# The second block's second mixer: a new order of its indexer, its latent attention and its output product

## The reference, cut to what matters

```python
def odd_mixer(x, w_in, q_norm_g, kv_norm_g, w_uq, w_ukv, w_o):
    qc, kc, vc, qi, ki, wi, cq, ckv, kr = split_cols(x @ w_in, ODD_SIZES)
    out_c = dsa_attention(qc(8 heads x 64), kc, vc, qi(4 x 64), ki, wi)
    q  = (rms_norm_2(cq, q_norm_g) @ w_uq)   # 8 heads x (64 + 32)
    kv = (rms_norm_2(ckv, kv_norm_g) @ w_ukv) # 8 heads x (64 + 64)
    q = concat([q[..., :64], rope(q[..., 64:], pos)])
    k = concat([kv[..., :64], rope(kr, pos) for every head])
    out_d = causal_block_attention(q, k, kv[..., 64:])
    return concat([out_c, out_d]) @ w_o
```

## Time and profile before

| | us |
|---|---|
| median of 3 runs | 2596.35 (2591.0 to 2599.19) |
| the profiled execution, its own time | 2602.1 |
| its span, first to last instruction | 2600.3 |
| PE busy in it | 2454.0 |
| DVE busy in it | 1727.7 |
| ACT busy in it | 1196.8 |
| mean granted clock of TensorE | 0.946 |

### The profile page before, as it was taken

One profiled execution on the slowest core, in us unless ns is written; L12 is line 12 of the kernel. 1 busy time (PEld: TensorE's weight loads), 2 busy tenths in 40 slices (PEclk: granted clock), 3 DMA queues, 4 the chain that ended last, 5 costly groups with the idle time before them and its releaser, 6 DMA issues.

```text
span 2600.3 us, 33971 instructions
## 1 busy us (share of the span) xinstructions
PE 2454.0 (94%) x14242; PEld 2109.2 (81%) x14242; DVE 1727.7 (66%) x2242; ACT 1196.8 (46%) x1493; POOL 98.7 (4%) x187
## 2 busy tenths in 40 slices
PE   6999999899999999999999999989999889899998
PEld 2778887767789999998899997867787767788776
DVE  4897776653656656655556655578787676588787
ACT  3212222343544444445444443466666544476565
POOL 0111111010000000000000000000000000000000
PEclk8999999999879999999899999999999886899999
DMA  6678787322114454456334543348887520298774
GB/s 270 220 236 265 263 267 249 123 87 77 65 65 163 172 194 168 167 194 224 109 144 177 191 162 113 102 161 301 315 315 300 208 97 23 103 350 323 274 301 187
DMA packets 80531, 502.23 MB, mean 193 GB/s; under 512 B 9621, under 2 KB 10725, under 8 KB 28513
## 3 DMA queue, kind: packets, MB, share of 16 engines
q1 hardware_dynamic: 59264, 424.71, 44.3%
q0 software_dynamic: 21088, 75.01, 9.1%
HBM read 498.63 MB, written 1.05 MB: 192 GB/s over the span
## 4 chain that ended last, share of the span: by engine, by line
PE 75%; DVE 14%; ACT 7%; issue 3%; DMA 1%; DVEq 0%; ACTq 0%; SPq 0%
PE bank L393 73%; DVE wl L1795 6%; ACT wh L1233 4%; DVE macc L1825 1%; PE bank L570 1%; ACT s L1318 1%; DVE f L1950 1%; DVE s L1941 1%; DMA raw<-in_wmod 1%; PE bank L1130 1%; DVE rs L1849 1%; DVE hl L1925 0%; DMA mring<-in_wmod 0%; ACT H L1327 0%; DVE tmpm L1918 0%
## 5 line engine op out<-in xcount | busy, mean ns | idle before, releaser
L1795 DVE TENSOR_TENSOR wl<-raw,wh 128x2048 fp32r<-128x2048 f32 x394 | 901.5, 2291 | 403.3 <-ACT wh L1233 400.8
L1233 ACT ACTIVATE wh<-raw 128x2048 fp32r<-128x2048 f32 x394 | 751.8, 1911 | 380.3 <-PE bank L393 379.0
L393 PE MATMUL bank<-hh,wh 128*128 128x258 f32 (+2 forms) x2200 | 694.5, 316 | 36.4 <-DVE wl L1795 18.4
L393 PE MATMUL bank<-hh,wl 128*128 128x258 f32 (+2 forms) x2200 | 678.8, 309 | 0.0
L393 PE MATMUL bank<-hl,wh 128*128 128x258 f32 (+2 forms) x2200 | 677.2, 308 | 0.0
L393 PEld LDWEIGHTS bank<-hh,wh 128*128 128x128 f32 x2200 | 424.9, 193 | 63.8 <-issue 18.0
L393 PEld LDWEIGHTS bank<-hl,wh 128*128 128x128 f32 x2200 | 425.8, 194 | 18.6
L393 PEld LDWEIGHTS bank<-hh,wl 128*128 128x128 f32 x2200 | 424.2, 193 | 19.2
L393 PE MATMUL bank<-wh,hh 128*128 128x512 f32 (+1 forms) x704 | 278.9, 396 | 5.2 <-DVE hl L2690 2.4
L393 PE MATMUL bank<-wh,hl 128*128 128x512 f32 (+1 forms) x704 | 274.3, 390 | 0.0
L393 PE MATMUL bank<-wl,hh 128*128 128x512 f32 (+1 forms) x704 | 274.3, 390 | 0.0
(11 more groups left out here) (421 smaller groups left out, 2760.1 us busy)
## 6 DMA issues: line engine op xcount, KB each, us to landing
raw<-in_wstream SPq DMA_DIRECT2D x394, 1024.0 KB, 4.9
mring<-in_wmod POOLq DMA_DIRECT2D x128, 512.0 KB, 4.6
raw<-in_wmod SPq DMA_DIRECT2D x8, 1024.0 KB, 9.3
X<-in_xT SPq DMA_DIRECT2D x1, 2048.0 KB, 12.5
bias<-in_nabias POOLq DMA_DIRECT2D x16, 128.0 KB, 2.5
c_sglg<-in_sglg POOLq DMA_DIRECT2D x1, 1024.0 KB, 5.2
c_sglb<-in_sglb POOLq DMA_DIRECT2D x1, 1024.0 KB, 7.4
out<-X SPq DMA_DIRECT2D x4, 256.0 KB, 2.2
```

The costliest lines, as they stand in the source:

```text
L393: return e.matmul(out, lhsT, rhs, start=start, stop=stop, skip_group_check=True)
L1233: e.activation(wh[i % NB][:], raw[i % NR][:], ACT.Copy).then_inc(*slab_high(i))
L1795: e.tensor_tensor(wl[i % NB][:], raw[i % NR][:], wh[i % NB][:].bitcast(F32), ALU.subtract).then_inc(*slab_low(i))
```

## The change

Packing. The columns of `w_uq` are reordered: four chunks of two heads' 64 unrotated parts (`od.qn`) and two chunks of four heads' rotated parts (`od.qr`), so `uq` takes 6 chunks instead of 8, and `ukvk` 4 instead of 8 (`od.kn`). The rotated key part is projected four times side by side, so that one rotation of 128 partitions serves it. The queries are rotated by one `rotate` over two chunks. The latent logits become two products into one bank, one of 64 rows (`qn`, `kn`) and one of 32 rows (`qr`, `kr`); `okf` goes. The mixer's tiles are now 80 + 12 + 4 + 4 + 24 (+ 4 empty) + 64, 12 slabs instead of 13.

Order. `ocq`, `ock`, `okr`, one `oqc` chunk and `okc` follow the indexer's columns, with selection steps between their tiles. The other three `oqc` chunks come after `ukvv`, with five attention steps in each (after tiles 1, 2, 4, 5, 7). All selection steps are run out before the first attention step (`pump(100)`). After the three chunks come 5 bare attention steps, then the transposes of the latent half of `Y` with a step after each, then 14 steps each behind two tiles of the half of w_o that needs only the latent half; the rest of w_o follows when the sparse half is done.

```diff
+OD_UNITS = (1, 2, 4, 5, 7)
@@ PE
+        def out_part(out, name, d, b, ks, first, last):
+            for k in ks:
+                w.wait_ge(dve_out, "turn l", name, k // 2)
+                wmm((out, d, k), b, hh[:, k, T:2 * T], hl[:, k, T:2 * T], k == first and (d > 5 or d % 2 == 0), k == last, out, d)
...
-            p(1, 11, "okr", 3)
-            p(2, 8, "ocq", 3)
-            p(1, 10, "ock", 3)
-            p(2, 0, "oqc", 1)
...
-            p(2, 2, "oqd", 1)
-            p(1, 4, "okc", 1)
+            p(2, 8, "ocq", pumps=True)
+            p(1, 10, "ock", pumps=True)
+            p(1, 11, "okr", pumps=True, middle=root_sum)
+            p(1, 0, "oqc", pumps=True)
             rotate(("rot", "kr"), od.kr[:].unsqueeze(1), act_out, "okr", 0)
+            p(1, 4, "okc", pumps=True)
...
+            q_part(4)
+            q_part(5)
+            for m in range(4):
+                q_part(m)
+                if m == 0:
+                    rotate(("rot", "qr"), od.qr, act_out, "uq", 5)
...
                 if kd == "la":
-                    w.wait_ge(dve_out, "okf")
-                    return mm(b[:, 0:n], od.qf[0:96, hd, P * qb:P * qb + P], od.kf[0:96, hd, 0:n], True, True)
+                    mm(b[:, 0:n], od.qn[r, hd // 2, q], od.kn[r, hd // 2, 0:n], True, False)
+                    r = slice(32 * (hd % 4), 32 * (hd % 4) + 32)
+                    return mm(b[:, 0:n], od.qr[r, hd // 4, q], od.kr[r, 0:n], False, True)
...
-            for _ in attention("od", OD, od.a, logits, values, (4, 5)):
-                pump(2)
-            for c in range(KC):
-                turn_out("od", od.Y, c)
-            out_proj("wo1", h_part, KC, ...)
+            pump(100)
+            st.units = attention("od", OD, od.a, logits, values, (4,))
+            p(3, 0, "oqc", m0=1, units=OD_UNITS)
+            pad()
+            attend(5)
+            for i in (2, 3):
+                turned(i, bank(("turn", "od", i), dve_out, "turn l", "od", i))
+                attend(1)
+            out_banks("wo1")
+            for d in range(6):
+                for k in (4, 6):
+                    part(d, where(d), k, k + 2)
+                    attend(1)
+            part(6, ends[0], 4, 6)
+            attend(1)
+            part(6, ends[0], 6, 8)
+            attend(1)
+            part(7, ends[1], 4, 6)
+            for i in (0, 1):
+                turned(i, bank(("turn", "od", i), dve_out, "turn l", "od", i))
+            part(7, ends[1], 6, 8)
+            sums_begin(2)
+            for d in range(KC):
+                part(d, where(d) if d < 6 else ends[d - 6], 0, 4)
+                if d > 1:
+                    sum_of(2, d - 2, "wo1", d - 2)
@@ ACT and DVE: the same order; DVE's loop over the 14 steps
+            for _ in range(14):
+                attend(1)
+                taken(2)
```

More of the change, by code:

```diff
@@ L429, in pad, with pad4 @@
                 st.tile += n
+        def pad4():
+            n = -st.tile % 4
+            order[-1].extend([None] * n)
+            st.tile += n
         def ended(ins, slab, last, key):
@@ L956, in h, with root_sum, p @@
                 return ("sp", 8, k)
-            def p(chunks, c0, key, steps=0):
-                for m in range(chunks):
+            def root_sum():
+                b = bank(("ossq",), dve_out, "omean")
+                for lo, n in ((0, 2), (2, 1)):
+                    for k in range(lo, lo + n):
+                        w.wait_ge(act_out, "osq", k)
+                        ins = mm(b[:, P * lo:P * lo + T], ones[:], od.lsq[:, k, :], k == lo, k == lo + n - 1)
+                ins.then_inc(*result("ossq"))
+            def p(chunks, c0, key, m0=0, pumps=False, units=(), middle=None):
+                for m in range(m0, m0 + chunks):
                     b = bank((key, m), act_out, key, m)
+                    st.kept.add(bank_of[key, m])
                     for k in range(KC):
@@ L963, in p @@
                         wmm(("oin", c0 + m, k), b[:, 0:T], hh[:, k, 0:T], hl[:, k, 0:T], k == 0, k == KC - 1, key, m)
-                    pump(steps)
-            st.selection = iter(())
+                        if pumps and k % 2:
+                            pump(1)
+                        if k in units:
+                            attend(1)
+                        if k == 3 and middle:
+                            middle()
+                    st.kept.remove(bank_of[key, m])
             p(1, 7, "oki")
@@ L1634, in odd_mixer, with root, high, p @@
             w.wait_ge(result, "moe 0")
-            def p(chunks, key, dst, scale=1.0, steps=0):
-                for m in range(chunks):
-                    taken(KC)
+            def root():
+                w.wait_ge(dve_out, "omean")
+                e.activation(rs[:], rs[:], ACT.Sqrt).then_inc(*act_out("oroot"))
+            def high():
+                for k in range(3):
+                    w.wait_ge(dve_out, "oc", k)
+                    e.activation(od.ch[:, k, :], od.cq[:, k, :], ACT.Copy).then_inc(*act_out("och", k))
+            def p(chunks, key, dst, scale=1.0, m0=0, pumps=False, units=0, middle=None):
+                for m in range(m0, m0 + chunks):
+                    taken(KC)
+                    if pumps:
+                        pump(4)
+                    attend(units)
+                    if middle:
+                        middle()
                     w.wait_ge(result, key, m)
                     e.activation(dst(m), banks[bank_of[key, m]][:, 0:T], ACT.Copy, scale=scale).then_inc(*act_out(key, m))
-                    pump(steps)
+            def query(m):
+                return od.qc[:, m, :]
             p(1, "oki", lambda m: od.ki[:])
@@ L2532, in odd_mixer @@
                                 ALU.add).then_inc(*dve_out("omean"))
-            for _ in range(2):
-                taken(KC)
-                pump(1)
+            pump(2)
             w.wait_ge(act_out, "oroot")
@@ L2566, in odd_mixer @@
+            pump(4)
+            for m in (4, 5, 0, 1, 2, 3):
                 taken(2)
+                if m == 0:
+                    behind()
+                    rotate(("rot", "qr"), od.qr)
                 pump(1)
-                if h % 2 and h > 1:
-                    rotate(("rot", h - 3), od.qf[:, h - 3:h - 1, :])
-            for h in range(8):
+            for m in range(4):
                 taken(1)
-                if h == 1:
-                    rotate(("rot", 6), od.qf[:, 6:8, :])
```

240 lines of the change are left out of this document (131 added, 109 removed).

## The result

The changed kernel takes 2615.83 us in the median (2598.06 to 2639.0, 10 runs), the kernel before 2595.39 beside it (2583.67 to 2609.94, 10 runs). The ratio is 1.0075, with a 95% interval of 1.0039 to 1.0112. The prediction was 2589.5, its range 2578 to 2604. A second measurement of the changed kernel gave 1.0113 [1.0038, 1.0188]. The profiled execution took 2608.53 us, its span is 2606.3.

A forecast was written before the change was run, and what follows sets the result against it. PE was taken as busy in 94% of the span, with DVE setting the pace before the attention. -20.4 us before the attention and +13.5 behind it take 6.9 off the median 2596.35: 2589.5 us, range 2578 to 2604.

The forecast's parts named there:

- Step 1, DVE's way: From DVE's copy of `ovw` to its first attention step: 43.8 us of work plus 4.4, reached 20.4 us earlier.
- The rival of a late start: Old DVE waits before the attention come back, up to 10 us, giving 2599.5; chance 0.14.
- My lower bound: DVE's earliest first attention step if there are no waits at all: 2124.5.
- Step 2, PE's work: PE's attention stage at the full clock: 61.7 us left from DVE's start; product pairs 0.42 on 128 keys, 0.63 on 256.
- Step 3(a) and (b), the waits: Attention stage waits: first exponentials 1.4 us; slab splits 5.3 in the second `oqc` chunk and 5.6 at tiles 128 and 144.
- The two of 2.8 at tiles 128 and 144: In the attention, slab splits between two loop steps leave PE waiting 2.8 us each time, 5.6 together.
- Step 3(d), the clock: In the attention, 10 to 15 us of PE's work runs at 1.2 GHz, costing 6 us more.
- The sum: -20.4 us before the attention, +13.5 behind it (97.4 to the last sum product, against 83.9): 6.9 off.
- The rival that came true: Attention stage stays at the half clock: +24 us over the whole stage, 2605 with two thirds slow; chance 0.16.
- the 8 us of standstills: In the half-clock rival's price, 8 of PE's 38 us of added work hide the split stalls.
- a cheap clock: Rival: clock and splits cost nothing in the attention, PE returns to 2.4 GHz at once; 6 us less, 2583.5; chance 0.20.
- Products side by side: Rival: the second latent product runs beside the first where row groups differ, 4.2 us less, 2585; chance 0.05.

The follow-up runs named there:

- `e_mask`: Changed kernel with every logit product on 128 rows, each head's key part in its own tile, zero elsewhere; 2589.98 us, 0.9964 of the kernel before.
- `e_rows`: Changed kernel with all logit products on 128 rows, two heads mixed in the logits (other values); 2585.44 us, 0.9953 of the kernel before.
- `e_96`: Changed kernel with all logit products on 96 rows from row 0, heads mixed; 2584.82 us, 0.9961 of the kernel before.
- `e_row0`: Changed kernel with logit products on as few rows as before but always from row 0, heads mixed; 2623.64 us, 1.0123 of the kernel before.
- `e_fill`: Changed kernel plus unused 128-row products, 40 in the first wait and four ahead of each unit's logits; 2613.61 us, 1.005 of the kernel before.

## Why the prediction was wrong, by its own steps

- **Step 1, DVE's way: right.** 48.2 us from the copy of `ovw` to the first attention instruction, forecast 48.1; five splits. The rival of a late start is out. (My lower bound is off by a little: 2078.6 + 43.8 + 2.4 of gaps is 2124.8, not 2124.5.)
- **Step 2, PE's work: the sizes were right at the full clock,** 0.42 and 0.63 per narrow product. What I didn't ask is why a second product should cost as much as the first. I took it for the price of a product; 0.2 of it is the change of rows, with a weight load that stands beside nothing. The way in and out, some 0.2 a step, I left out.
- **Step 3(a) and (b), the waits: half right.** PE's standstill in the second chunk was forecast at 5.3 and is 4.96, in its place and ended by an exponential. The first exponentials were forecast at 1.4 and are 1.35 (2108.97 to 2110.32). The two of 2.8 at tiles 128 and 144 don't show in the changed kernel, where PE at half the clock is always late; with the clock up `e_mask` has 2.29 and 3.00 there.
- **Step 3(d), the clock: this is the step that failed.** "With tiles between the steps I take 10 to 15 us of PE's work at 1.2 GHz." It was all of the stage, 108.6 us. I had read the earlier trace rows as a matter of how busy PE is and what stands around it: attention brought the clock back at 2163, so attention plus tiles would sooner. (The prediction calls it sparse attention; by the rows it was the latent one.) But the rows also say which products were which: those at 2152 to 2163 had 96 rows, those of 2178 to 2203, at 97% busy and 0.50, had 64. The change turned the first sort into the second sort and a third (32 rows). The clock fell at the end of the DVE-bound stage (0.98 in 2103 to 2109, 0.50 from 2109), and this mix of steps and tiles doesn't bring it back; with wide rows and the same steps and tiles it comes back (`e_rows`, `e_96`, `e_mask`).
- **The sum.** From the first attention step to the last sum product I forecast 97.4 us, bounds 92 to 103; measured 133.2. In `e_mask` it is 94.3 (2131.33 to 2225.6), so rows are 38.9 of it: 10 to 16 for the changes of rows, of which my sizes held 9.6 already, and 23 to 29 for the clock. That is the net of the standstills which slower work hides: PE is idle in the attention for 6.4 us here and 14.6 in `e_mask`, and its busy time is 102.2 against 54.05, 48.2 more, of which over 30 are the clock's. So one term decides: 3(d) was sized 6 where it is 23 at the least, and above 30 in PE's own work. Without the 9.6 my working would give 87.8 for `e_mask`; its 6.5 more I haven't split, but it has a wait that my list lacks, 2.4 us for DVE's part of the split of `Y`.
- **The rival that came true** is the half clock throughout. I had given it 0.16 and priced the whole stage at +24; it is +35.8 on the 97.4. Of the 8 us of standstills that I let it hide only the two of 2.8 went, that of 4.96 stayed, and the way in and out of narrow products was in no size. By its own price it would have given 2589.5 + 24 = 2613.5, outside my range; the measured 2615.83 lies close to that, in part by luck, as the stretch missed the price by 12 us. That it would hold for only two thirds of the stage was too mild as well. My reason for a cheap clock, that the first mixer holds 2.4 GHz with four tiles between steps, counted tiles and not rows.
- **Products side by side:** none. The Trainium skill, in "TensorE: Matmul & The Clock Gate", Part 3, says that weight loads overlap with running products only when the row group differs; the same part also lets a load go ahead into the background weight buffer. Here 128 rows after 128 rows overlap (0.22 us ahead), and so does the second load of a narrow product, on the same 64 rows as the first (2134.06 and 2134.49), while 32 rows after 64 don't, in other rows or, in `e_row0`, from the same row 0. The page's closing table says that a product on 32 rows takes the same time as one on 128; in these fp32 pairs it takes 0.63 against 0.43.

What stays open: whether the clock looks at the rows themselves, at the loads that stand alone, or at the changes of rows. All three switch together between 64 and 96 rows, and no run has narrow products of one row count behind one another. `e_fill` has the lone loads still (0.63 per product) and the clock at 0.86, so they don't forbid the full clock if enough full-row work stands beside them. Nor do narrow products by themselves: the kernel before is granted 1.00 from 2168.9 to 2177.6 with 64-row products on 128 keys and falls as those on 256 begin, and the first mixer is granted 1.00 from 1640 to 1676 with pairs of 64 and 8 rows and four tiles between steps. How much narrow work it takes, no run tells.

## What to carry to other kernels

In these fp32 products a contraction on 64 rows or fewer was no smaller job than one on 128: it was longer by its change of rows, with the weight load unhidden, and where such products filled much of the stage TensorE stayed at 1.2 GHz while PE was 94% busy. Fill the rows (with zeros in place of the other head, one tile per head) before thinking of the order, and when a busy PE shows a granted clock of 0.50, look at the rows in the shape column. And put work that needs no partner where an engine already waits for another one, here the DVE-bound stage, not into a circle of three engines that runs well by itself.

## What the hardware showed that I had not expected

- In this stage rows decide the clock by a step: the same program at 64, 32 and 64 rows takes 108.6 us at 0.50 (`e_row0`), at 96 rows 68.1 at 0.88, at 128 rows 68.2 at 0.88.
- Rows of zeros count in full: `e_mask` is granted 0.87, mixed heads 0.88.
- A narrow product takes 0.42 and 0.63 us on 128 and 256 keys where a wide one takes 0.22 and 0.43, at the same 2.4 GHz.
- The weight load that stood unhidden is the one at a change between 128, 64 and 32 rows; the second load of the same narrow product runs 0.43 us ahead (2134.06 and 2134.49).
